# Block 1 attention of a two-block fp32 transformer: another order for head pairs 4 to 7 among the engines

## The reference, cut to what matters

```python
q = (_rms_norm(x, g_norm) @ w_q).reshape(b, n_chunks, CHUNK, B_HEADS, B_HEAD_DIM)   # 16 heads of 64
...
sc = jnp.einsum('bqhd,bkhd->bhqk', q_c, k_c).astype(jnp.float32) * ATTN_SCALE + bias
valid = (c * CHUNK + key_offset) >= 0
sc = jnp.where(valid, sc, NEG_INF)
p = jax.nn.softmax(sc, axis=-1).astype(v_c.dtype)
return jnp.einsum('bhqk,bkhd->bqhd', p, v_c)
...
return o @ w_o
```

## The kernel before, in words

| step | engine | what it does | what it waits for |
|---|---|---|---|
| `scores(p)` L1721 | PE | q k of two heads, into PSUM banks tb0 and tb1 | bias step of pair p-1 |
| `pair_begin(p)` L1125 to L1132 | DVE | scale and bias into `sb1`, negated maxima | the scores; the turn of pair p-2 (two buffers of `sb1`); the bias in `rb` |
| `pair_exp(p)` L655 | ACT | four exps with row sums | the maxima |
| `pair_norm(p)` L1137, L1141 | DVE | times one over the sums | the exps |
| `p_turn(p)` L1531 | PE | six transposes into tb2 and tb3 | `pair_norm(p)` and `y_lo(p-1)` |
| `pair_keep(p)` L660, L662 | ACT | into `pt1` | the transposes |
| `pv(p)` L1740 | PE | probabilities by v | `pair_keep(p)`; from pair 4 on also `v_keep(3)` |
| `y_hi(p)` L666 | ACT | high part of o | `pv(p)` |
| `y_lo(p)` L1147 | DVE | low part of o | `y_hi(p)` |

## Time and profile before

### The profile page before, as it was taken

The page is one execution under the profiler, slowest core; times in us unless marked ns, Lnnn a source line. Parts: engine busy times, 40 slices in busy tenths (PEclk is TensorE's granted clock), DMA queues, the critical chain, the costliest instruction groups (busy, mean ns, idle before and its releaser), DMA issues.

```text
span 1268.7 us, 16607 instructions
## 1 busy us (share of the span) xinstructions
PE 1245.9 (98%) x6276; PEld 1027.1 (81%) x6276; DVE 816.0 (64%) x926; ACT 664.3 (52%) x800; POOL 141.7 (11%) x164
## 2 busy tenths in 40 slices
PE   7999999999999989999999999999999999999998
PEld 5888888888898768888887788888888777888886
DVE  5466455545567565555469976777746987687763
ACT  6545264434366554444347356676536554666652
POOL 2000000000010000000029610000003930000000
PEclk9999999999999999999999999999999999999999
DMA  9544454446364236445634235544562424554440
GB/s 346 211 182 179 170 197 178 169 186 232 133 249 154 96 122 240 170 170 216 225 112 161 100 129 203 199 161 170 185 223 103 166 95 166 199 183 157 189 183 33
DMA packets 32534, 220.13 MB, mean 174 GB/s; under 512 B 4000, under 2 KB 4032, under 8 KB 6752
## 3 DMA queue, kind: packets, MB, share of 16 engines
q1 hardware_dynamic: 29952, 212.35, 45.2%
q0 software_dynamic: 1664, 5.41, 1.4%
q10 hardware_dynamic: 864, 1.61, 0.4%
HBM read 218.31 MB, written 1.05 MB: 173 GB/s over the span
## 4 chain that ended last, share of the span: by engine, by line
PE 95%; DVE 3%; ACT 1%; DMA 0%; issue 0%; POOLq 0%; POOL 0%; ACTq 0%
PE acc L1499 28%; PE acc L1501 27%; PE acc L1500 27%; PE tb L1531 5%; DVE wlo L947 1%; PE acc L1686 1%; PE acc L1688 1%; PE acc L1689 1%; DVE cacc L1246 1%; PE tb L1859 1%; PE tb L1600 1%; PE tb L1721 1%; PE acc L1885 0%; PE tb L1740 0%; PE acc L1891 0%; DMA x<-in_x_in 0%
## 5 line engine op out<-in xcount | busy, mean ns | idle before, releaser
L947 DVE TENSOR_TENSOR wlo<-raw,whi 128x2048 fp32r<-128x2048 f32 x200 | 458.1, 2310 | 237.4 <-ACT whi L489 237.4
L489 ACT ACTIVATE whi<-raw 128x2048 fp32r<-128x2048 f32 x200 | 376.8, 1907 | 109.2 <-PE acc L1501 100.9
L1499 PE MATMUL acc<-whi,xth 128*128 128x512 f32 (+1 forms) x1056 | 419.1, 397 | 4.4 <-DVE xtl L969 2.2
L1501 PE MATMUL acc<-whi,xtl 128*128 128x512 f32 (+1 forms) x1056 | 409.2, 387 | 0.0
L1500 PE MATMUL acc<-wlo,xth 128*128 128x512 f32 (+1 forms) x1056 | 408.4, 387 | 0.0
L1499 PEld LDWEIGHTS acc<-whi,xth 128*128 128x128 f32 x1056 | 198.7, 188 | 50.0 <-issue 5.8
L1501 PEld LDWEIGHTS acc<-whi,xtl 128*128 128x128 f32 x1056 | 198.6, 188 | 41.3
L1500 PEld LDWEIGHTS acc<-wlo,xth 128*128 128x128 f32 x1056 | 199.0, 188 | 36.8
L1499 PE MATMUL acc<-whi,yth 128*128 128x512 f32 x512 | 202.2, 395 | 1.7 <-DVE ytl L1380 1.7
L1501 PE MATMUL acc<-whi,ytl 128*128 128x512 f32 x512 | 199.7, 390 | 0.0
L1500 PE MATMUL acc<-wlo,yth 128*128 128x512 f32 x512 | 199.5, 390 | 0.0
(11 more groups left out here) (238 smaller groups left out, 1030.2 us busy)
## 6 DMA issues: line engine op xcount, KB each, us to landing
raw<-in_stream SPq DMA_DIRECT2D x200, 1024.0 KB, 4.8
rb<-in_rel_rows POOLq DMA_DIRECT2D x8, 256.0 KB, 2.9
raw<-in_stream SPq DMA_DIRECT2D x4, 256.0 KB, 4.9
raw<-in_stream SPq DMA_DIRECT2D x2, 512.0 KB, 8.1
gs_sb<-in_gs_row POOLq DMA_DIRECT2D x1, 1024.0 KB, 5.4
frow<-in_fin_row POOLq DMA_DIRECT2D x2, 512.0 KB, 5.4
x<-in_x_in ACTq DMA_DIRECT2D x2, 256.0 KB, 5.0
x<-in_x_in ACTq DMA_DIRECT2D x1, 512.0 KB, 7.3
```

The costliest lines, as they stand in the source:

```text
L489: act.activation(whi[:, s, :], raw[:, s, :], ACT.Copy).then_inc(hi_ready, 1)
L947: dve.tensor_tensor(wlo[:, s, :], raw[:, s, :], whi[:, s, :], ALU.subtract).then_inc(lo_ready, 1)
L1499: pe.matmul(o, xh, wh, start=first, stop=False)
L1501: return pe.matmul(o, xl, wh, start=False, stop=last)
```

## The change

It changes no operation, no buffer and no wait. It moves calls within the written orders of three engines, all in the stretch of pairs 4 to 7.

```diff
@@ ScalarE
             pair_keep(3)
             pair_exp(4)
             y_hi(3)
+            pair_exp(5)
             v_keep(2)
             pair_keep(4)
-            pair_exp(5)
+            hi(U_WO + 2)
+            pair_exp(6)
             v_keep(3)
             y_hi(4)
-            hi(U_WO + 2)
             pair_keep(5)
-            pair_exp(6)
+            pair_exp(7)
             y_hi(5)
+            hi(U_WO + 3)
             pair_keep(6)
-            pair_exp(7)
-            hi(U_WO + 3)
+            hi(U_WO + 4)
             y_hi(6)
+            hi(U_WO + 5)
             pair_keep(7)
             y_hi(7)
-            hi(U_WO + 4)
-            hi(U_WO + 5)
             norm(3)
@@ VectorE
             pair_begin(5)
             pair_norm(5)
-            y_lo(4)
             pair_begin(6)
             lo(U_WO + 2)
+            pair_norm(6)
+            y_lo(4)
+            pair_begin(7)
+            pair_norm(7)
             y_lo(5)
-            pair_norm(6)
-            pair_begin(7)
             lo(U_WO + 3)
             y_lo(6)
-            pair_norm(7)
-            y_lo(7)
             lo(U_WO + 4)
             lo(U_WO + 5)
+            y_lo(7)
             norm(3)
@@ TensorE
-            v_step(1, m0={1: lambda: p_turn(3), 3: lambda: scores(4), 5: lambda: pv(3)},
-                   m1={3: lambda: (scores(5), p_turn(4))})
+            v_step(1, m0={0: lambda: scores(4), 1: lambda: p_turn(3), 4: lambda: pv(3), 5: lambda: scores(5)},
+                   m1={1: lambda: p_turn(4), 4: lambda: scores(6)})
...
-                (0, 0): lambda: pv(4), (0, 1): lambda: scores(6), (0, 2): lambda: p_turn(5),
-                (1, 0): lambda: (pv(5), scores(7)), (1, 1): lambda: p_turn(6), (1, 3): lambda: pv(6), (2, 0): lambda: p_turn(7), (2, 2): lambda: pv(7)})
+                (0, 0): lambda: pv(4), (0, 1): lambda: (p_turn(5), scores(7)), (0, 3): lambda: pv(5),
+                (1, 0): lambda: p_turn(6), (1, 2): lambda: pv(6), (1, 3): lambda: p_turn(7), (2, 1): lambda: pv(7)})
```

## The result

| | before | after |
|---|---|---|
| runs measured together | 6 | 6 |
| time, median | 1271.69 us | 1266.32 us |
| lowest to highest | 1270.46 to 1273.14 | 1265.79 to 1266.49 |
| span of the profiled execution | 1268.7 us | 1264.6 us |
| W (below) | 52.80 us | 48.05 us |

The ratio is 0.9955, 95% interval 0.9944 to 0.9965: the kernel is faster, by 5.4 us in the medians. The forecast was 1266.9, with 4.8 us less.

The account below looks back on a forecast made before the run. TensorE bounds the kernel, on the chain for 95% of the span. Stalls gone 5.65 us, added 0.86, net 4.8 less from a base of 1271.7: 1266.9 us, own range 1264.5 to 1268.9 (8 in 10: 1264.4 to 1270.6).

Parts of the forecast that it names:

- W: Time from the first triple of the second v step to the gated layer's first matmul; net forecast 4.8 us less.
- stall before the turn of pair 3: TensorE's wait for pair 3's normalisation; scores of pair 4 moved ahead of that turn remove 0.67 us.
- stall before the turn of pair 7: TensorE's wait there; earlier scores of pair 7 and pair_norm(7) ahead of the split of WO+3 remove 3.10 us.
- stall before the norm's first turn: TensorE's wait there; the two last weight splits moved ahead of y_lo(7) remove 1.88 us.
- new wait before pv(4): TensorE waits for v_keep(3), now behind pair_exp(6) on ScalarE: 0.62 us added, bounds 0 and 1.77.
- before the turn of pair 6: TensorE waits for y_lo(5), now behind pair_norm(7) on VectorE: 0.04 us added, bounds 0 and 1.2.
- pv and scores parted: On TensorE, pair 5's pv and pair 7's scores no longer stand together: 0.20 us added.
- the second and third parts: Earlier scores(7) and pair_norm(7), credited 3.10 us; two last weight copies and splits ahead of y_lo(7), credited 1.88 us.
- The rival of copies on the path: ScalarE's three moved copies get waited for, giving back 1.8 to 3.6 us: 1268.7 to 1270.5 us; chance 0.12.
- the cover that the prediction worked out: 0.5 us spare before pv(7) with hi(U_WO + 5) ahead of pair_keep(7) on ScalarE; cost 0, else up to 1.3.
- The rival of VectorE's queue: Late y_lo steps behind other VectorE work hold TensorE, up to 9.2 us added, 4.4 us slower, 1276 us; chance 0.05.
- the margin that I called nil: Turn of pair 6: y_lo(5) ready 6.14 us after scores(7) start, TensorE needs 6.10 us.

Follow-up runs that it names:

- VectorE's order alone: Old kernel with only pair_norm(7) and y_lo(6) moved ahead of the split of WO+3 on VectorE: 1267.97 us, ratio 0.9962.
- another such pair: Changed kernel with pv(3) moved beside scores(5), both after kt 5: one run, 1265.45 us.
- the undoings: Changed kernel with pair_norm(7) back behind the split of WO+3 (1266.49 us), or with the two last copies and splits back behind y_hi(7) and y_lo(7) (1266.49 us).

## Why the prediction was right

| term | forecast | measured |
|---|---|---|
| stall before the turn of pair 3 | -0.67 | gone; alone in the old kernel the bracket goes too |
| stall before the turn of pair 7 | -3.10 | gone; -3.02 in W by VectorE's order alone |
| stall before the norm's first turn | -1.88 | gone |
| new wait before pv(4) | +0.62 | +0.71; removing it gives 0.66 of W |
| before the turn of pair 6 | +0.04 | +0.11, too little for a bracket |
| pv and scores parted | +0.20 | +0.23 for another such pair |
| W | -4.8 | -4.75 |

The mechanism was right, and each term to within 0.1 us. The step before it, that the ends of matmuls are modelled and a bracket hides a further 0.16 us, mattered: 5.17 would have been read where 5.65 was lost. The new wait is the term that was sized least well. From the start of scores(6) at 423.11 to pv(4) at 428.30 it is 5.19 us, not 5.12, and TensorE was ready after 4.48; the bracket was forecast as some 0.5 and is 0.64.

The near equality of 4.8 and 4.75 is in part two small errors that cancel. The forecast puts 0.86 us on the adding side, the trace 1.08: 0.71, 0.11, 0.20, and 0.06 for scores(5) and a turn that were parted, which the sum took as 0. On the other side the sum left out that the turn behind a stall takes some 0.07 us longer itself, as the rows show: 0.88, 0.88 and 0.66 us in the earlier trace rows, and 0.82, 0.82 and 0.60 in the changed kernel. Three times 0.07 is some 0.20. The three stalls themselves come to 5.63 us by the starts of the matmuls on both sides of each (0.67, 3.09 and 1.87), and 5.63 + 0.20 - 1.08 = 4.75. The range of the gain, 4.2 to 5.9, is not worked out from the bounds of the terms: with both new waits at nothing they give 5.45 at most, and with both at their upper bounds some 2.5.

Single starts came less exactly than the net. With the 0.6 us of the late start taken off, the bias step of pair 7 comes at 431.7 (forecast 431.6), the two last splits at 442.2 and 445.0 (441.9 and 444.7), the first add at 451.6 (451.2) and the gated layer at 457.0 (456.7 carried through, 457.0 with the 0.25 us allowed).

One point in the change's account was only half right. I gave the second and third parts their whole stalls. Together they do remove them, but the undoings show that the parts overlap: pair 7's normalisation is free where I credited its move, and the splits are worth 0.58 us beside the earlier pv(7).

What the sum lacked is the clock, and that the forecast of the time came within 0.6 us is in part luck. I took the scatter of the old kernel's runs (1270.46 to 1273.14) as noise and its mean, 1271.7, as the base. It is two groups, and the upper is the same stall's second price. The changed kernel has no long stall, and its six runs lie within 0.7 us. From the old kernel's lower group (1270.46 to 1270.57 in the six runs measured with the result) the gain to the new median is some 4.2 us; W's 4.75 less a late start of 0.6, as seen in the profile, would give that, but the starts of the other executions were not read. From its upper group (1272.81 to 1273.14) it is 6.6. The median, 5.4, lies between. The forecast of 4.8 came near this because the base held half of the second price already; the profile, with a granted clock of 1.00 everywhere, came from an execution of the lower group and could not show it.

The rival of copies on the path did not happen, but one copy did hold a step up. ScalarE's rows of `hi(U_WO + 5)` and `pair_keep(7)`:

```profile
443.69 1.92 ACT L489 ACTIVATE whi<-raw 128x2048 fp32r<-128x2048 f32 x1 [1.28 <-PE acc L1501]
445.51 0.57 ACT L660 ACTIVATE pt<-tb 128x512 f32<-128x512 f32 x1
```

The turn of pair 7 started at 443.43, so by the step of 0.69 us the keep could have started at 444.12; it stood 1.4 us behind the copy. It was still over before pv(7) at 446.95, within the cover that the prediction worked out, and TensorE waited for nothing. `y_hi(6)` (442.02) found ScalarE idle. The rival of VectorE's queue did not happen either, but the margin that I called nil is nil.

## What to carry to other kernels

Where engines take their work in a written order, carry the start of each step through the new order with durations from the trace: here it gave the net of a change on three engines to within 0.1 us and single starts to within 0.4, with the one new wait in the right place. Read for each moved step what now stands ahead of it on its own engine, since that is where both the cures and the new waits were (one line moved on VectorE gave 3.0 of the 4.75 us). And look at the runs before the mean: two groups of times in a kernel with one long TensorE stall can be the clock, and then the stall is worth more than its length. Filling the stall with useless matmuls is a test for that.

## What the runs showed of the hardware

- At a stall of 2.93 to 3.72 us TensorE's granted clock fell to 0.50 (1.2 GHz instead of 2.4), in three of the four profiles with such a stall: 0.5 us after its end in one, 0.6 us before it in the second, 1.5 us before it in the third (the stall of 3.72 us). In the fourth, the old kernel's own, it stayed at 1.00. The cost in W was 1.55 us in one of them, 1.3 in the second and 2.2 to 2.4 in the third, and 2.4 us lie between the means of the two groups of the old kernel's runs.
- The transposes of a turn take 0.06 to 0.07 us longer right behind a stall (0.88 against 0.82 us for six, 0.66 against 0.60 for four).
- Keeping TensorE busy with useless matmuls through the stall avoided it: 1270.69 us against 1272.50.
- Executions differ by up to 1.2 us before the first 153 us are over (the norm's first turn of the first product at 152.30 to 153.48 us in 14 profiles, whose kernels are the same up to there), by how long the first matmuls take 0.63 us instead of 0.39. Differences below a microsecond are to be read from a stretch of the trace, not from the span.
